# Fp32r matmuls of an encoder block: sixteen stationary tiles put 264 columns apart instead of 256, and attT on the weight tiles' remainder modulo 512 bytes

## The chip, the cores and the metric

The kernel runs on one core of one Trainium2 chip. The metric is the device time of one execution in microseconds (us); the times shown are of three executions.

## The reference

One layer of an encoder over 256 tokens with a model width of 2048, in float32:

```python
x = x + 0.5 * swiglu(rms_norm(x, norm_ffn1_w[l]), ffn1_w_gate[l], ffn1_w_up[l], ffn1_w_down[l])
x = x + head_group_mixer(rms_norm(x, norm_mix_w[l]), w_in[l], attn_sinks[l], ret_gn_w[l], w_out[l])
x = x + 0.5 * swiglu(rms_norm(x, norm_ffn2_w[l]), ffn2_w_gate[l], ffn2_w_up[l], ffn2_w_down[l])
...
return rms_norm(x, norm_final_w)
```

`swiglu` is `(silu(h @ w_gate) * (h @ w_up)) @ w_down` with an inner width of 5632. The mixer projects to 5376 columns, runs sliding-window attention (16 heads) on one half and retention (4 heads) on the other, and projects 2048 columns back with `w_out`.

## The kernel before, in words

Every large product is computed as three float32r matmuls per tile. An operand a is split into a high part and the remainder, a_lo = a - a_hi, and the product is a_hi·w_hi + a_hi·w_lo + a_lo·w_hi, all three accumulated in one PSUM bank. The helper `half` (lines 313 to 322) issues this for two k tiles (j) and two token tiles (t): 2 x 2 x 3 = 12 matmuls on lines 319, 320 and 321. In each, the **stationary** operand (what LDWEIGHTS puts into the array) is a 128 x 128 piece of the activations, and the **moving** operand is a row of 512 weight columns (448 in the input projection).

Four families of SBUF tiles hold the stationary pieces. `xT_hi` and `xT_lo` are the transposed, weighted x, 16 k tiles of 256 columns each; they serve gate, up and the input projection with tiles 0 to 15, and their upper eight tiles serve the retention half of `w_out`. `hT_hi` and `hT_lo` (4 k tiles) serve the down projections. `attT_hi` and `attT_lo` (8 k tiles) serve the attention half of `w_out` and, through `last_hT_hi` and `last_hT_lo`, the last down step of either FFN (`last_down`, lines 389 to 422, which in the second FFN issues its own matmuls on lines 419 to 421). A token tile is 128 float32 columns, 512 bytes, so t does not change an address modulo 512.

Weights come by DMA in pieces of 1 MB into `raw` (SP's queue, line 248), four slots; ScalarE copies half a slot into `w_hi` (line 613, rounding it to float32r) and VectorE subtracts to get `w_lo` (line 812). Both have four slots (`LEAD`), each of two rows of 512 columns, 2048 bytes a row. `half` waits on `lo_ready` for its slot and increments `half_used`, on which ScalarE waits before it overwrites the slot. The order of everything is written out by hand; TensorE runs gate and up of FFN step i, then down of step i - 1, with transposes (line 325) between them.

SBUF tensors are laid out one behind the other in the order in which `build` asks for them (line 77). The small tensors and the filler `to_line` end so that x, xT_hi, xT_lo, raw, w_hi and w_lo all begin at byte 0 modulo 512; each of these has a size that is a multiple of 512 bytes per partition. So have proj, cos, sin, junk, decay, hT_hi, hT_lo and the attention tiles behind them. The filler `off_line` (32 float32, 128 bytes) stands ahead of attT_hi, so attT_hi and attT_lo begin at byte 128 modulo 512.

Of the kernel before, what the change touches and what calls it, by code (L numbers as in the profile page):

```python
# [20 lines left out]
P = 128  # L21
D = 2048
SEQ = 256
T = SEQ // P
KT = D // P
# [17 lines left out]
RAW = 4  # L43
LEAD = 4
HALF = 2 * W


G_FFN = [0, 3 * NF + NI + 4]
# [19 lines left out]
F32R = mybir.dt.float32r  # L68
# [3 lines left out]
def build(nc, x_d, norms_d, g1, u1, d1, w_in, sinks_d, gn_d, w_out, g2, u2, d2, fw_d, ident_d, cos_d, sin_d,  # L72
          decay_d, out_d):
    ffn_w = [(g1, u1, d1), (g2, u2, d2)]
    with ExitStack() as ctx:
        def sb(name, shape, dt=F32, stack=ctx):
            return stack.enter_context(nc.sbuf_tensor(name, shape, dt))
# [23 lines left out]
        mv = sb("mv", [P, RH, T, 2])  # L101
        var_eps = sb("var_eps", [P, RH, T])
        gn_rstd = sb("gn_rstd", [P, RH, T])
        sb("to_line", [P, 32])


        x = sb("x", [P, T, D])
        xT_hi = sb("xT_hi", [P, KT, SEQ], F32R)
        xT_lo = sb("xT_lo", [P, KT, SEQ], F32R)
        raw = sb("raw", [P, RAW, 4 * W])  # L110
        w_hi = sb("w_hi", [P, LEAD, 2, W], F32R)
        w_lo = sb("w_lo", [P, LEAD, 2, W], F32R)
# [18 lines left out]
        probs = sb("probs", [P, T, QUAD, P])  # L131
        probsT = sb("probsT", [P, T, QUAD * P])
        att = sb("att", [P, T, QUAD * HD])
        sb("off_line", [P, 32])
        attT_hi = sb("attT_hi", [P, KT // 2, SEQ], F32R)
        attT_lo = sb("attT_lo", [P, KT // 2, SEQ], F32R)

# [94 lines left out]
        def f32(ap):  # L232
            return ap.bitcast(F32)
# [8 lines left out]
        def _(sp):  # L242
# [39 lines left out]
            for i, (kt0, kt1) in enumerate(X_PIECES):  # L282
                cols = slice(kt0 * P, kt1 * P)
                sp.dma_start(x[:, :, cols], xv[:, :, cols]).then_inc(x_loaded[i], 16)
                if i < 2:
                    sp.dma_start(raw[:, 0, i * HALF:(i + 1) * HALF].rearrange("p (k c) -> p k c", k=2),
                                 g1[2 * P * i:2 * P * (i + 1), 0:W].rearrange("(k p) c -> p k c", p=P)
# [313 lines left out]
        def _(act):  # L601
            def split(g, k, first=False):
# [9 lines left out]
                dst = w_hi[:, k % LEAD, :, :].rearrange("p k c -> p (k c)")  # L612
                act.activation(dst, raw[:, s, (k % 2) * HALF:(k % 2 + 1) * HALF], ACT.Copy).then_inc(hi_ready, 1)  # L613

# [191 lines left out]
        def _(dve):  # L806
            def split(g, k):
# [4 lines left out]
                dve.tensor_tensor(w_lo[:, k % LEAD, :, :].rearrange(flat),  # L812
                                  raw[:, k // 2, (k % 2) * HALF:(k % 2 + 1) * HALF],
                                  f32(w_hi[:, k % LEAD, :, :].rearrange(flat)), ALU.subtract).then_inc(lo_ready, 1)
# [364 lines left out]
```

## Time and profile before

| | |
|---|---|
| three runs, median (lowest to highest) | 1848.09 us (1847.88 to 1848.19) |
| the profiled execution's own time | 1848.02 us |
| its span, first to last instruction | 1846.2 us |
| mean granted TensorE clock | 0.999 |
| TensorE busy (PE) | 1835.1 us, 99% |
| weight loads busy (PEld, beside PE) | 1541.2 us, 83% |
| VectorE, ScalarE, GpSimd busy | 1045.5, 831.8, 64.2 us |
| HBM read | 341.95 MB, 186 GB/s over the span |

A row of a group of instructions gives line, engine, operation, output and inputs, shape and count, then the busy time in us and the mean duration of one in ns. Matmuls are pipelined, so a duration is longer than the distance to the next one; the distance from start to start is what one matmul costs, and the timeline view shows it.

### The profile page before, as it was taken

Reading aid. Unit: us, or ns where it says so; the run is one execution under the profiler, and the core shown is the slowest. Engines: PE = TensorE matmul, PEld = TensorE weight load, DVE = VectorE, ACT = ScalarE, POOL = GpSimd, SP = SyncE. Lnnn points to the kernel's source line nnn. Section 1 sums busy time; section 2 is a strip of 40 time slices with the busy share of each in tenths; the row PEclk is TensorE's granted clock in tenths of the full one; section 3 lists DMA queues with packets and bytes.
Section 4 is the critical chain, followed back from the end, with each engine's and each line's share of the span. In section 5 each row is a group of like instructions: output and inputs, shape, how many; then the busy total and the mean of one; then the engine's idle time right before and its main releaser. Section 6 shows DMA issues by size and latency. Waiting matters only on the chain.

```text
span 1846.2 us, 23124 instructions
## 1 busy us (share of the span) xinstructions
PE 1835.1 (99%) x8602; PEld 1541.2 (83%) x8602; DVE 1045.5 (57%) x1087; ACT 831.8 (45%) x995; POOL 64.2 (3%) x59
## 2 busy tenths in 40 slices
PE   9999999999999999999999999999999999999998
PEld 7888888888888888999998888888888888888886
DVE  5555565555556556655557665555555555546546
ACT  6444444444443444555555445443444444444344
POOL 0000000000000000000009000000000000000000
PEclk9999999999999999999999999999999999999999
DMA  8556556555555555564555456556556556555552
GB/s 312 192 183 200 185 184 202 182 191 195 184 195 190 187 198 173 165 194 160 163 174 177 140 171 210 190 183 202 183 185 201 182 192 194 184 193 190 189 198 92
DMA packets 176898, 344.53 MB, mean 187 GB/s; under 512 B 5984, under 2 KB 31456, under 8 KB 176736
## 3 DMA queue, kind: packets, MB, share of 16 engines
q1 hardware_dynamic: 176864, 344.07, 56.8%
q8 instruction: 23, 0.38, 0.1%
q14 instruction: 11, 0.09, 0.0%
HBM read 341.95 MB, written 2.10 MB: 186 GB/s over the span
## 4 chain that ended last, share of the span: by engine, by line
PE 99%; issue 0%; DMA 0%; DVE 0%; ACT 0%; SPq 0%; POOLq 0%; POOL 0%; DVEq 0%
PE ps L319 32%; PE ps L321 32%; PE ps L320 32%; PE ps L325 2%; PE ps L450 0%; PE ps L534 0%; PE ps L545 0%; DMA raw<-in_g 0%; PE ps L463 0%; PE ps L421 0%; PE ps L420 0%; PE ps L419 0%; DVE x L861 0%; DVE proj L1047 0%; DVE w_lo L812 0%
## 5 line engine op out<-in xcount | busy, mean ns | idle before, releaser
L812 DVE TENSOR_TENSOR w_lo<-raw,w_hi 128x1024 fp32r<-128x1024 f32 x656 | 812.8, 1241 | 762.4 <-ACT w_hi L613 761.2
L613 ACT ACTIVATE w_hi<-raw 128x1024 fp32r<-128x1024 f32 x656 | 695.2, 1061 | 972.8 <-PE ps L321 970.6
L319 PE MATMUL ps<-w_hi,xT_hi 128*128 128x512 f32 (+1 forms) x1856 | 718.3, 387 | 0.5 <-DVE w_lo L812 0.5
L321 PE MATMUL ps<-w_hi,xT_lo 128*128 128x512 f32 (+1 forms) x1856 | 713.3, 384 | 0.0
L320 PE MATMUL ps<-w_lo,xT_hi 128*128 128x512 f32 (+1 forms) x1856 | 713.1, 384 | 0.0
L319 PEld LDWEIGHTS ps<-w_hi,xT_hi 128*128 128x128 f32 x1856 | 348.6, 188 | 63.8 <-issue 1.9
L321 PEld LDWEIGHTS ps<-w_hi,xT_lo 128*128 128x128 f32 x1856 | 348.5, 188 | 63.3
L320 PEld LDWEIGHTS ps<-w_lo,xT_hi 128*128 128x128 f32 x1856 | 348.7, 188 | 61.7
L319 PE MATMUL ps<-w_hi,hT_hi 128*128 128x512 f32 x640 | 249.1, 389 | 0.0
L321 PE MATMUL ps<-w_hi,hT_lo 128*128 128x512 f32 x640 | 249.0, 389 | 0.0
L320 PE MATMUL ps<-w_lo,hT_hi 128*128 128x512 f32 x640 | 249.0, 389 | 0.0
L321 PEld LDWEIGHTS ps<-w_hi,hT_lo 128*128 128x128 f32 x640 | 120.2, 188 | 24.9
L320 PEld LDWEIGHTS ps<-w_lo,hT_hi 128*128 128x128 f32 x640 | 120.2, 188 | 24.8
L319 PEld LDWEIGHTS ps<-w_hi,hT_hi 128*128 128x128 f32 x640 | 120.2, 188 | 24.8
L861 DVE SCALAR_TENSOR_TENSOR x<-ps,x 128x512 f32<-128x512 f32 x188 | 120.3, 681 | 0.3 <-PE ps L321 0.3
L1054 POOL TENSOR_TENSOR rstd<-ms_eps,minus_half 128x2 f32<-128x2 f32 (+1 forms) x5 | 4.1, 827 | 1520.4 <-DVE ms_eps L835 1520.4
L319 PE MATMUL ps<-w_hi,attT_hi 128*128 128x512 f32 x112 | 45.9, 409 | 0.0
L321 PE MATMUL ps<-w_hi,attT_lo 128*128 128x512 f32 x112 | 44.2, 395 | 0.0
L320 PE MATMUL ps<-w_lo,attT_hi 128*128 128x512 f32 x112 | 44.2, 394 | 0.0
L824 DVE SCALAR_TENSOR_TENSOR xT_lo<-ps,norms,xT_hi 128x256 fp32r<-128x256 f32 x48 | 20.4, 477 | 20.0 <-ACT xT_hi L623 20.0
L845 DVE SCALAR_TENSOR_TENSOR h<-ps,rstd,sg 128x512 f32<-128x512 f32 x44 | 30.8, 742 | 0.0
L623 ACT ACTIVATE xT_hi<-ps,norms 128x256 fp32r<-128x256 f32 x48 | 19.3, 473 | 19.6 <-PE ps L325 19.6
(100 smaller groups left out, 526.0 us busy)
## 6 DMA issues: line engine op xcount, KB each, us to landing
raw<-in_u SPq DMA_DIRECT2D x88, 1024.0 KB, 5.1
raw<-in_d SPq DMA_DIRECT2D x88, 1024.0 KB, 4.9
raw<-in_g SPq DMA_DIRECT2D x87, 1024.0 KB, 5.1
raw<-in_w_in SPq DMA_DIRECT2D x48, 896.0 KB, 4.6
raw<-in_w_out SPq DMA_DIRECT2D x16, 1024.0 KB, 4.9
out<-proj SPq DMA_DIRECT2D x8, 256.0 KB, 2.4
x<-in_x SPq DMA_DIRECT2D x3, 512.0 KB, 9.5
raw<-in_g SPq DMA_DIRECT2D x2, 512.0 KB, 5.5
```

The source lines that it names most:

```text
L319: pe.matmul(out, xh, wh, start=first and j == 0, stop=False)
L320: pe.matmul(out, xh, wl, start=False, stop=False)
L321: mm = pe.matmul(out, xl, wh, start=False, stop=last and j == 1)
L325: return pe.transpose(ps[0:src.shape[1], bank, col:col + P], src, ident[:])
L613: act.activation(dst, raw[:, s, (k % 2) * HALF:(k % 2 + 1) * HALF], ACT.Copy).then_inc(hi_ready, 1)
L623: a = act.activation(xT_hi[:, kt, :], ps[:, x_bank(norm, p), j * SEQ:(j + 1) * SEQ], ACT.Copy, scale=norms[:, norm, kt:kt + 1])
L812: dve.tensor_tensor(w_lo[:, k % LEAD, :, :].rearrange(flat), raw[:, k // 2, (k % 2) * HALF:(k % 2 + 1) * HALF], f32(w_hi[:, k % LEAD, :, : ...
L824: a = dve.scalar_tensor_tensor(out=xT_lo[:, kt, :], in0=ps[:, x_bank(norm, p), j * SEQ:(j + 1) * SEQ], scalar=norms[:, norm, kt:kt + 1], i ...
L845: dve.scalar_tensor_tensor(out=h[:, t, :], in0=ps[:, B_UP + t, :], scalar=rstd[:, (FFN1, FFN2)[f], t:t + 1], in1=sg[:, t, :], op0=ALU.mult ...
L861: a = dve.scalar_tensor_tensor(out=xb, in0=ps[:, B_DOWN + 2 * (n % 2) + t, :], scalar=scale, in1=xb, op0=ALU.mult, op1=ALU.add)
L1054: pool.tensor_tensor(rstd[:, norm, t0:t1], ms_eps[:, norm, t0:t1], minus_half[:, t0:t1], ALU.pow).then_inc(rstd_ready, 1)
```

## The change

The rows of xT_hi and xT_lo become 264 columns (1056 bytes) long, of which the first 256 are used. k tile number n therefore begins 32·n bytes further modulo 512 than k tile 0. Both tensors grow by 16 x 32 = 512 bytes, so what stands behind them keeps its remainder relative to them. `to_line` loses 32 bytes, so x, xT_hi, xT_lo (tile 0), raw, w_hi, w_lo and the rest begin at byte 480 modulo 512. `off_line` goes, so attT begins at 480 too, as the weight tiles do. No instruction is added, removed or moved on any engine.

| | before, bytes modulo 512 | after |
|---|---|---|
| w_hi, w_lo, raw, hT, proj | 0 | 480 |
| xT, k tile n | 0 | 480 + 32·n |
| attT | 128 | 480 |
| xT relative to w | 0 | 32·n |
| hT relative to w | 0 | 0 |
| attT relative to w | 128 | 0 |

```diff
+STEP = 8
...
-        sb("to_line", [P, 32])
+        sb("to_line", [P, 24])
...
-        xT_hi = sb("xT_hi", [P, KT, SEQ], F32R)
-        xT_lo = sb("xT_lo", [P, KT, SEQ], F32R)
+        xT_hi = sb("xT_hi", [P, KT, SEQ + STEP], F32R)[:, :, 0:SEQ]
+        xT_lo = sb("xT_lo", [P, KT, SEQ + STEP], F32R)[:, :, 0:SEQ]
...
-        sb("off_line", [P, 32])
         attT_hi = sb("attT_hi", [P, KT // 2, SEQ], F32R)
         attT_lo = sb("attT_lo", [P, KT // 2, SEQ], F32R)
```

## Rows read from the trace of the kernel before

**Rows 1.** The page's first part and the granted clock by slice

```profile
PE 1835.1 (99%) x8602; PEld 1541.2 (83%) x8602; DVE 1045.5 (57%) x1087; ACT 831.8 (45%) x995; POOL 64.2 (3%) x59
...
PEclk9999999999999999999999999999999999999999
```

**Rows 2.** The chain that ended last, shares by engine and by line

```profile
PE 99%; issue 0%; DMA 0%; DVE 0%; ACT 0%; SPq 0%; POOLq 0%; POOL 0%; DVEq 0%
PE ps L319 32%; PE ps L321 32%; PE ps L320 32%; PE ps L325 2%; PE ps L450 0%; PE ps L534 0%; PE ps L545 0%; DMA raw<-in_g 0%; PE ps L463 0%; PE ps L421 0%; PE ps L420 0%; PE ps L419 0%; DVE x L861 0%; DVE proj L1047 0%; DVE w_lo L812 0%
```

**Rows 3.** Groups of instructions, shapes apart: matmuls by stationary tile

```profile
L319 PE MATMUL ps<-w_hi,xT_hi 128*128 128x512 f32 x1472 | 576.0, 391 | 0.5 <-DVE w_lo L812 0.5
...
L319 PE MATMUL ps<-w_hi,hT_hi 128*128 128x512 f32 x640 | 249.1, 389 | 0.0
...
L319 PE MATMUL ps<-w_hi,xT_hi 128*128 128x448 f32 x384 | 142.3, 371 | 0.0
...
L319 PE MATMUL ps<-w_hi,attT_hi 128*128 128x512 f32 x112 | 45.9, 409 | 0.0
...
L419 PE MATMUL ps<-w_hi,attT_hi 128*128 128x512 f32 x16 | 6.3, 394 | 0.0
```

**Rows 4.** Timeline (start us, duration us), a matmul beside the next load

```profile
1102.18 0.39 PE L319 MATMUL ps<-w_hi,xT_hi 128*128 128x512 f32 x1
1102.19 0.19 PEld L320 LDWEIGHTS ps<-w_lo,xT_hi 128*128 128x128 f32 x1
```

**Rows 5.** Timeline, TensorE: xT against w, first and last of 24 matmuls

```profile
1074.78 0.39 PE L320 MATMUL ps<-w_lo,xT_hi 128*128 128x512 f32 x1
...
1080.00 0.39 PE L319 MATMUL ps<-w_hi,xT_hi 128*128 128x512 f32 x1
```

**Rows 6.** Timeline, TensorE: hT against w, first and last of 24 matmuls

```profile
1399.68 0.39 PE L320 MATMUL ps<-w_lo,hT_hi 128*128 128x512 f32 x1
...
1404.90 0.39 PE L319 MATMUL ps<-w_hi,hT_hi 128*128 128x512 f32 x1
```

**Rows 7.** Timeline, TensorE: attT against w, first and last of 23 matmuls

```profile
1815.76 0.40 PE L319 MATMUL ps<-w_hi,attT_hi 128*128 128x512 f32 x1
...
1820.88 0.40 PE L320 MATMUL ps<-w_lo,attT_hi 128*128 128x512 f32 x1
```

**Rows 8.** Timeline, TensorE: attT in the first FFN, first and last of 14 matmuls

```profile
739.80 0.40 PE L320 MATMUL ps<-w_lo,attT_hi 128*128 128x512 f32 x1
...
742.84 0.39 PE L321 MATMUL ps<-w_hi,attT_lo 128*128 128x512 f32 x1
```

**Rows 9.** Timeline, TensorE: 448 columns, xT against w, first and last of 27

```profile
752.64 0.36 PE L321 MATMUL ps<-w_hi,xT_lo 128*128 128x448 f32 x1
...
757.91 0.36 PE L320 MATMUL ps<-w_lo,xT_hi 128*128 128x448 f32 x1
```

**Rows 10.** bf16 warm-up matmuls: three in the timeline, and the tile's durations (min/median/max ns)

```profile
8.25 0.81 PE L559 MATMUL ps<-junk 128*128 128x512 bf16 x3
...
L559 PE MATMUL ps<-junk x14: 379/631/631, 1.5 to 8.7; 128*128 128x512 bf16 x14
```

**Rows 11.** The two splits, and who waited for whom (us in total, times, longest)

```profile
L812 DVE TENSOR_TENSOR w_lo<-raw,w_hi 128x1024 fp32r<-128x1024 f32 x656 | 812.8, 1241 | 762.4 <-ACT w_hi L613 761.2
L613 ACT ACTIVATE w_hi<-raw 128x1024 fp32r<-128x1024 f32 x656 | 695.2, 1061 | 972.8 <-PE ps L321 970.6
...
ACT w_hi L613 <- PE ps L321: 970.6, 609, 3.5
...
ACT w_hi L613 <- DMA raw<-in_g: 0.7, 2, 0.4
...
raw<-in_u SPq DMA_DIRECT2D x88, 1024.0 KB, 5.1
```

## The prediction

> **What bounds the kernel now.** I read the page's first part first. TensorE is busy for 1835.1 us of the 1846.2 us span, and the granted clock is at its upper level, 2.4 GHz, in every slice [rows 1]. The chain of waits says the same: 99% of it lies on TensorE, and 96% on lines 319 to 321, the three products of `half` [rows 2]. So the time is the number of those matmuls times what one costs from start to start, and nothing that the change does elsewhere counts unless it comes to hold TensorE up.
>
> The groups with shapes kept apart give the numbers [rows 3]; each of the three lines has the same counts. Stationary from xT: 1472 x 3 = 4416 matmuls of 512 columns and 384 x 3 = 1152 of 448. From hT: 640 x 3 = 1920. From attT: 112 x 3 and, in the second FFN's last step, 16 x 3, together 384.
>
> The durations in these groups are of pipelined matmuls, so for the cost of one I go to the timeline and divide the distance between two starts by the number of steps:
>
> - xT, 512 columns: (1080.00 - 1074.78) / 23 = 0.2270 us [rows 5]
> - hT, 512 columns: (1404.90 - 1399.68) / 23 = 0.2270 us [rows 6]
> - attT, 512 columns: (1820.88 - 1815.76) / 22 = 0.2327 us [rows 7], and (742.84 - 739.80) / 13 = 0.2338 us in the first FFN [rows 8]
> - xT, 448 columns: (757.91 - 752.64) / 26 = 0.2027 us [rows 9], where 448/512 of 0.2270 would be 0.1986 us.
>
> This is the pair on which everything rests. hT and attT are used in down steps of the same shape, with the same moving operand and the same clock. They differ in where they stand: hT on the weight tiles' remainder modulo 512, attT 128 bytes past it. The second costs 5.7 ns more for each matmul. The timeline also shows why the two operands can meet: the load of the next stationary tile starts 0.01 us after the matmul it runs beside, and takes 0.19 of its 0.227 us [rows 4]. Both read SBUF at once.
>
> **The change, part by part.** No instruction is added or moved, so all of it is in the cost of one matmul.
>
> 1. *attT on the weights' remainder.* Its 384 matmuls come from 0.2327 to hT's 0.2270 us: 384 x 5.7 ns = 2.2 us less, all on the path. If another reason made attT slow, it is 0.
>
> 2. *xT's k tiles 1 to 15 off the weights' remainder*, by 32, 64, ... 480 bytes. Tile 0 stays on it. Gate and up take every tile equally often, and so does the input projection; the retention half of `w_out` takes tiles 8 to 15 alone. The matmuls of xT in the FFNs are 4416 less the 64 x 3 of `w_out`, 4224; with the projection's 1152 there are 5376, of which a sixteenth, 336, stays. So 5568 - 336 = **5232 matmuls** get a distance that is not 0.
>  Of the fifteen distances the trace shows one: 128, which is tile 4's, at 5.7 ns [rows 6, 7]. The bound above is worse than that: 0.2338 us, 6.8 ns for each [rows 5, 8], 5232 x 6.8 = 35.6 us. The bound below is a gain. The bf16 warm-up matmuls also stream 512 columns beside a load: three of them take 0.81 us with the last one's 0.379, so (0.81 - 0.379) / 2 = 0.2155 us [rows 10]. That is 11.5 ns below 0.2270, and 5232 x 11.5 = 60.2 us less if every distance reached it.
>  I take half of attT's price, 2.85 ns: among the distances some lie near 0 in either direction and some near or beyond 128, and the two that the trace shows cost 0 and 5.7. That is 5232 x 2.85 = **14.9 us more**, all on the path. For 448 columns I use the same figure; they already cost 4.1 ns more than in proportion [rows 5, 9], which says that a distance of 0 is no guarantee, and could cut both ways.
>
> 3. *Everything else now at remainder 480.* For hT the distance stays 0; I take 0. The splits on ScalarE and VectorE take 1061 and 1241 ns [rows 11] of the 12 x 0.227 = 2.72 us of a half, which leaves each of them over 1.4 us of a half, and ScalarE idles 970.6 us in all waiting for TensorE [rows 11]; either could take twice as long and stay hidden. If that cover went, TensorE would wait for `lo_ready`. A weight piece lands in 5.1 us, its slot is wanted again about six halves or 16 us later, and ScalarE waited only 0.7 us in all for one [rows 11]: a landing in raw at another remainder is hidden up to three times its time. ScalarE's and VectorE's writes of xT's tiles are one tile each, so the gaps cost them nothing; their bound is the same cover.
>
> The sum: 14.9 - 2.2 = +12.7 us. The profiled execution took 1848.02 us (span 1846.2 and 1.8 around it), as good as the median 1848.09, so 1848.1 + 12.7 = **1860.8 us**.
>
> One rule speaks against any effect. The Trainium skill, in "TensorE: Matmul & The Clock Gate" (step-by-step: what each phase is for), says that TensorE has two independent SBUF read ports, so that loading the next weights takes no read bandwidth from the running matmul; by it both terms would be 0 and the time 1848. The trace disagrees as far as its 5.7 ns between attT and hT go. The same page gives 215.7 ns between matmuls of 512 columns (back-to-back issue gap), and the warm-up's 0.2155 us agrees; the fp32r matmuls here stand 11 ns above it.
>
> **The rivals.**
>
> - *Every distance costs what 128 costs.* Then the term is 5232 x 5.7 = 29.8 us, the sum +27.6 and the time 1875.7 us. For it: attT is the one row off the remainder. Against: it is one distance of fifteen.
> - *The spread relieves the reads (faster).* At distance 0 the two streams start on the same remainder at the same moment [rows 4], and each of these matmuls stands 11.5 ns above the warm-up's. If that is a collision in each of them, some distances avoid it. With half of the matmuls, 2616, at 0.2155 us and the rest unchanged: 2616 x 11.5 = 30.1 us less, with attT's 2.2 less, 1815.8 us. It is decided by the mean over xT's distances: below 0.2270 us the kernel gains there, and with attT's part break-even lies 0.4 ns above it (2.2 / 5232). For it: nothing else in the rows explains why fp32r costs 11 ns more than bf16. Against: the only distance seen off 0 is worse, not better.
> - *The distance does nothing*, and attT is slow for a reason that goes with it or stays, such as its place far behind in SBUF. Then 1848.1 us, or 1845.9 with attT's part. Against it: nothing else differs between hT's and attT's matmuls.
> - *It is the remainder itself that counts, not the distance:* whatever does not begin at a multiple of 512 pays 5.7 ns. Then hT pays as well: (5568 + 1920) x 5.7 = 42.7 us, attT gains nothing, and the time is 1890.8 us. The rows can't exclude it, since all that stands at distance 0 also stands at byte 0.
> - That the change does not do what it says would need a tensor between xT and w_hi whose size is no multiple of 512; there is none (16896, 32768 and 16384 bytes).
>
> **How the numbers follow.** A measurement of this kernel can tell 0.2%, some 3.7 us, from no change. Forecast 0.33; every distance as 128: 0.17; relief 0.33; nothing 0.10; remainder itself 0.07. Faster is 0.33, within 0.2% 0.10, slower 0.33 + 0.17 + 0.07 = 0.57. Cases of both signs are open. The forecast's own range is 1850 to 1882 us (between hardly any cost and the upper bound, 1848.1 + 35.6 - 2.2 = 1881.5). The range of 8 in 10 reaches up to 1884 us, which leaves out the remainder itself (0.07), and down to 1812 us, which takes in the relief case down to a little below its worked value and leaves out the third of it, about 0.11, in which nearly every distance reaches the warm-up's figure.
>
> **What would show it.** In the changed kernel's timeline attT's matmuls should stand 0.227 us apart, and hT's still 0.227. Within a gate or up step the distance should change from one k tile to the next, since each brings 6 matmuls of one distance: tile 0 at 0.227, tile 4 near 0.233. A tile below 0.227 shows relief; all tiles at 0.233, the first rival; hT at 0.233, the remainder itself. VectorE's and ScalarE's splits should keep 1241 and 1061 ns. The prediction is wrong if the mean over the k tiles is below 0.2270 us, or if TensorE shows waits on `w_lo` that it does not have now.

## The result: 1.3% slower, and the profile after

| | before | after |
|---|---|---|
| runs, median (lowest to highest), us | 1848.09 (1847.88 to 1848.19) | 1872.66 (1872.51 to 1872.88) |
| ratio, with its 95% interval | | 1.0131 (1.0119 to 1.0144) |
| span of the profiled execution, us | 1846.2 | 1871.1 |

The changed kernel takes 24.6 us longer. It lies inside the range of 1812 to 1884 us, on the side that had 0.57, but twice as far from 1848 as the forecast of 1860.8 us. The first rival, every distance at attT's old price, gave 1875.7 us and is nearer.

The page of the kernel after shows the same amount of work in a longer span, at the same clock:

```profile
PE 1859.8 (99%) x8602; PEld 1541.0 (82%) x8602; DVE 1046.1 (56%) x1087; ACT 832.2 (44%) x995; POOL 63.3 (3%) x59
...
PEclk9999999999999999999999999999999999999999
...
L812 DVE TENSOR_TENSOR w_lo<-raw,w_hi 128x1024 fp32r<-128x1024 f32 x656 | 813.3, 1241 | 787.2 <-ACT w_hi L613 786.0
L613 ACT ACTIVATE w_hi<-raw 128x1024 fp32r<-128x1024 f32 x656 | 695.8, 1062 | 998.1 <-PE ps L321 995.0
```

TensorE has 24.7 us more busy time, the loads have none, and the two splits keep their 1241 and 1062 ns against [rows 11]. ScalarE's idle time in front of line 613 grew by 25 us: it waits longer for TensorE, as everything does. So the cost lies in the matmuls alone.

The timeline of TensorE of the kernel after, one up projection of the second FFN. These are the starts of k tiles 0, 1, 6, 7, 14 and 15 (6 matmuls each) and, behind them, the first matmul of the down step:

```profile
1661.60 0.40 PE L319 MATMUL ps<-w_hi,xT_hi 128*128 128x512 f32 x1
...
1662.99 0.40 PE L319 MATMUL ps<-w_hi,xT_hi 128*128 128x512 f32 x1
...
1669.98 0.40 PE L319 MATMUL ps<-w_hi,xT_hi 128*128 128x512 f32 x1
...
1671.36 0.40 PE L319 MATMUL ps<-w_hi,xT_hi 128*128 128x512 f32 x1
...
1681.15 0.40 PE L319 MATMUL ps<-w_hi,xT_hi 128*128 128x512 f32 x1
...
1682.53 0.40 PE L319 MATMUL ps<-w_hi,xT_hi 128*128 128x512 f32 x1
...
1683.93 0.40 PE L319 MATMUL ps<-w_hi,hT_hi 128*128 128x512 f32 x1
```

The same pass of the kernel before:

```profile
1638.99 0.39 PE L319 MATMUL ps<-w_hi,xT_hi 128*128 128x512 f32 x1
...
1660.75 0.39 PE L319 MATMUL ps<-w_hi,hT_hi 128*128 128x512 f32 x1
```

The pass of 96 matmuls took 21.76 us, 0.2267 us each, and now takes 22.33 us, 0.2326 us each. Within it the price follows the tile. Tile 6 (192 bytes off) has 1.38 / 6 = 0.230 us and tile 14 (448 bytes off) the same; tile 15 has 1.40 / 6 = 0.233. Tile 0, whose distance is 0, has 1.39 / 6 = 0.232 and not 0.2267. There are 44 such passes (gate and up, 11 steps, two FFNs): 44 x 0.57 = 25.1 us by this one pass. Over all passes of the kernel after, tile 0 has a mean of 229.9 ns and tile 8, which is 256 bytes off, 231.1; tile 4, 128 bytes off, has 232.5, and in the kernel before the mean over all tiles is 226.9 (gaps over 300 ns, in which TensorE waited or did something else, left out).

The tiles with the unchanged distance, and attT. First hT in a down step of the kernel after (34 matmuls), then attT in the last step of the second FFN (first and last of 22):

```profile
1428.79 0.39 PE L321 MATMUL ps<-w_hi,hT_lo 128*128 128x512 f32 x1
...
1436.27 0.39 PE L321 MATMUL ps<-w_hi,hT_lo 128*128 128x512 f32 x1
...
1841.23 0.39 PE L319 MATMUL ps<-w_hi,attT_hi 128*128 128x512 f32 x1
...
1845.99 0.39 PE L319 MATMUL ps<-w_hi,attT_hi 128*128 128x512 f32 x1
```

hT stands at 7.48 / 33 = 0.2267 us as in [rows 6], although it now begins at byte 480. attT went from 0.2327 us [rows 7] to 4.76 / 21 = 0.2267.

Summed over the whole of either trace, each matmul counted from its start to the next one's start (so with what waiting there was), the families have:

| stationary tile, moving columns | before, us | after, us | difference, us |
|---|---|---|---|
| xT, 512 (4416 matmuls) | 1005.1 | 1029.9 | +24.8 |
| xT, 448 (1152) | 236.5 | 237.1 | +0.7 |
| hT, 512 (1920) | 435.4 | 436.0 | +0.6 |
| attT, 512 (383 of 384 are in the trace) | 90.7 | 89.2 | -1.5 |

Together +24.6 us. The profiled spans differ by 24.9, and the other 0.3 us lie in the warm-up matmuls ahead of the work.

### The profile page after: what moved, and what is told of

It is laid out like the page before. It is cut to its first block, busy times and chain, and to the rows that moved or that the text cites. A ratio compares the mean times of both kernels' runs of the same rounds, so it can differ in the third digit from the quotient of the medians.

```text
span 1871.1 us, 23124 instructions
## 1 busy us (share of the span) xinstructions
PE 1859.8 (99%) x8602; PEld 1541.0 (82%) x8602; DVE 1046.1 (56%) x1087; ACT 832.2 (44%) x995; POOL 63.3 (3%) x59
## 4 chain that ended last, share of the span: by engine, by line
PE 99%; issue 0%; DMA 0%; DVE 0%; ACT 0%; SPq 0%; POOLq 0%; POOL 0%; DVEq 0%
PE ps L319 32%; PE ps L321 32%; PE ps L320 32%; PE ps L325 2%; PE ps L450 0%; DMA raw<-in_g 0%; PE ps L534 0%; PE ps L545 0%; PE ps L463 0%; PE ps L421 0%; PE ps L419 0%; PE ps L420 0%; DVE x L861 0%; DVE proj L1047 0%; DVE w_lo L812 0%
## 5 line engine op out<-in xcount | busy, mean ns | idle before, releaser
L812 DVE TENSOR_TENSOR w_lo<-raw,w_hi 128x1024 fp32r<-128x1024 f32 x656 | 813.3, 1241 | 787.2 <-ACT w_hi L613 786.0
L613 ACT ACTIVATE w_hi<-raw 128x1024 fp32r<-128x1024 f32 x656 | 695.8, 1062 | 998.1 <-PE ps L321 995.0
L319 PE MATMUL ps<-w_hi,xT_hi 128*128 128x512 f32 (+1 forms) x1856 | 727.0, 392 | 0.4 <-DVE w_lo L812 0.4
L321 PE MATMUL ps<-w_hi,xT_lo 128*128 128x512 f32 (+1 forms) x1856 | 721.7, 389 | 0.0
```

Source lines behind the costliest of these rows:

```text
L319: pe.matmul(out, xh, wh, start=first and j == 0, stop=False)
L321: mm = pe.matmul(out, xl, wh, start=False, stop=last and j == 1)
L812: dve.tensor_tensor(w_lo[:, k % LEAD, :, :].rearrange(flat), raw[:, k // 2, (k % 2) * HALF:(k % 2 + 1) * HALF], f32(w_hi[:, k % LEAD, :, : ...
```

## The experiments

All runs were compared with the kernel before on the same chip; its median was 1848.28, 1848.56 and 1848.26 us in the three groups of runs. Times are medians, except that each run with added series is one execution, read from its trace alone.

### Parts of the change, one at a time

**attT's share alone.**

```diff
-        sb("off_line", [P, 32])
```

> The filler ahead of attT goes and nothing else: attT at distance 0 from the weight tiles, xT at distance 0 as before. Theory A (the distance between stationary and moving operand modulo 512 bytes sets the cost of a matmul): attT's 384 matmuls come from 0.2325 to about 0.227 us, the kernel to 1845.9 us, and this is the share of the changed kernel's time that was a gain. Rival B (attT was slow for its place or for its neighbours in the program): nothing changes, 1848.1 us.

Measured: 1846.9 us against 1848.28, ratio 0.9991 (0.9982 to 1.0). Its timeline has attT, first and last of 24 matmuls, 5.21 / 23 = 0.2265 us apart:

```profile
1814.73 0.39 PE L318 MATMUL ps<-w_hi,attT_hi 128*128 128x512 f32 x1
...
1819.94 0.39 PE L320 MATMUL ps<-w_hi,attT_lo 128*128 128x512 f32 x1
```

The price per matmul moved as theory A has it. The total gained 1.4 us where 2.2 were expected, and the interval of the ratio just reaches 1, so the total alone would not settle it. The trace does: from start to start attT's matmuls take 89.1 us in all instead of 90.7, 1.6 us less. (All matmul lines stand one line higher here, since one line of the source is gone.)

**Everything at byte 480, all distances 0.**

```diff
-        sb("to_line", [P, 32])
+        sb("to_line", [P, 24])
...
-        sb("off_line", [P, 32])
```

> As the run before it, and to_line 32 bytes shorter, so that x, xT, raw, w_hi, w_lo, hT, attT all begin at byte 480 modulo 512, at distance 0 from each other. Theory A (distance alone): the same as the run before it, 1845.9 us. Rival C (it is the remainder 480 itself that costs): matmuls at 0.2327 us everywhere, about +43 us, near 1889 us. The changed kernel's hT at 0.227 us speaks for A already.

Measured: 1848.46 us, ratio 1.0001 (0.9992 to 1.001), with single runs from 1847.58 to 1850.69. Rival C falls: nothing near 43 us. It is 1.6 us above the run before it, which theory A did not have. In the profiled executions the distance is 3.1 us (1849.51 and 1846.37), and it lies in the 448-column matmuls, which take 239.6 us in all instead of 236.6. There are 30 steps between these two rows of the timeline, 0.2067 us each:

```profile
769.77 0.37 PE L318 MATMUL ps<-w_hi,xT_hi 128*128 128x448 f32 x1
...
775.97 0.37 PE L318 MATMUL ps<-w_hi,xT_hi 128*128 128x448 f32 x1
```

The kernel before has 0.2027 for the same shape at the same distance [rows 9]. This second price of one geometry comes back in the series below.

**All xT tiles at one distance, 256 bytes.**

```diff
+        sb("gap", [P, 64])
         raw = sb("raw", [P, RAW, 4 * W])
...
-        sb("off_line", [P, 32])
```

> xT's tiles stand 256 columns apart as before, all sixteen at one distance of 256 bytes from the weight tiles (a filler of 256 bytes between xT_lo and raw); attT and hT at distance 0. Theory A: xT's matmuls of 512 columns at about 0.2325 us, 4416 x 5.7 ns = +25 us on the run with attT alone, near 1871 us. Rival D (the price of the changed kernel comes from the change of distance between one k tile and the next, not from the distance): 0.227 us for xT, 1846 us. Rival E (half way round the line the two reads are farthest apart and don't meet): xT's matmuls below 0.227 us, down to 0.216, 1846 - 49 = 1797 us.

Measured: 1846.78 us, ratio 0.9992 (0.9983 to 1.0001). In its trace the matmuls of xT with 512 columns take 1005.1 us, as in the run with attT alone (1005.0). By itself this looked like rival D, and the theory that any distance costs 5.7 ns was wrong. The series settled which.

### The price of each distance

**Series with fixed distances.** Behind the last down step, TensorE goes on with matmuls on what the weight buffers hold; their results are left out of the output:

```diff
             ffn(1)
+            def series(cols, offs, n, still=P):
+                for c in offs:
+                    for i in range(n):
+                        pe.matmul(ps[0:still, i % 2, 0:cols], w_hi[:, 0, 0, c:c + still], w_lo[:, 1, 0, 0:cols],
+                                  start=True, stop=True)
+            series(512, range(0, 136, 8), 32)
+            series(448, range(0, 136, 8), 24)
+            series(512, range(1, 8), 24)
+            series(512, (0,), 24, 64)
```

> The kernel before with extra fp32r matmuls on TensorE behind its last down step (their result is not used, the total time is some 260 us longer and says nothing). Each series has one distance between the stationary tile (128 columns of w_hi) and the moving row (w_lo): 0, 32, 64, ... 512 bytes with 32 matmuls of 512 columns each, the same distances with 24 of 448 columns each, then 4, 8, ... 28 bytes with 24 of 512 columns, then distance 0 with a stationary tile of 64 columns. Theory A: 0.227 us at 0 and 512 bytes, about 0.232 at all others. Rival D: 0.227 at every distance, since none changes within a series. Rival E: a curve with a low place, below 0.227, somewhere. With 64 stationary columns, if it is the load's reads that the moving operand meets, about half of the 11 ns above the warm-up's 0.2155 us should go: 0.221 us; if fp32r has a fixed cost, 0.227.

The timeline merges the matmuls of one line, so a window over the settled part of a series gives one row: start, then the time from its first start to its last end. With the last one's 0.39 us (512 columns) taken off and the rest divided by the count less one, that is the price. The 512-column series at 0, 32, 64, 96, 128, 160, 192, 224 and 256 bytes:

```profile
1840.39 5.84 PE L602 MATMUL ps<-w_lo,w_hi 128*128 128x512 f32 x25
...
1847.69 5.99 PE L602 MATMUL ps<-w_lo,w_hi 128*128 128x512 f32 x25
...
1855.16 5.99 PE L602 MATMUL ps<-w_lo,w_hi 128*128 128x512 f32 x25
...
1862.62 6.01 PE L602 MATMUL ps<-w_lo,w_hi 128*128 128x512 f32 x25
...
1870.10 5.97 PE L602 MATMUL ps<-w_lo,w_hi 128*128 128x512 f32 x25
...
1877.54 5.99 PE L602 MATMUL ps<-w_lo,w_hi 128*128 128x512 f32 x25
...
1884.97 5.89 PE L602 MATMUL ps<-w_lo,w_hi 128*128 128x512 f32 x25
...
1892.33 5.99 PE L602 MATMUL ps<-w_lo,w_hi 128*128 128x512 f32 x25
...
1899.75 5.84 PE L602 MATMUL ps<-w_lo,w_hi 128*128 128x512 f32 x25
```

| distance, bytes | 0 | 32 | 64 | 96 | 128 | 160 | 192 | 224 | 256 |
|---|---|---|---|---|---|---|---|---|---|
| 512 columns, ns | 227.1 | 233.3 | 233.3 | 234.2 | 232.5 | 233.3 | 229.2 | 233.3 | 227.1 |

From 256 to 512 bytes the rows repeat to the hundredth of a microsecond. So distance does have a price, also where it never changes, and rival D falls as the only cause. But the price repeats every **256 bytes, not 512**; that is why the kernel with 256 bytes lost nothing. With 512 columns no distance that was tried is cheaper than 0. Distances of 4 to 28 bytes cost 230.6 to 235.0 ns, so 32 bytes is not the grain either. The 232.5 ns at 128 bytes are attT's old 232.7 [rows 7]; the mean over eight steps of 32 bytes is 232.0 ns.

A series needs some matmuls to settle. The first six steps of the series at distance 0 take 235, 225, 230, 236, 229 and 232 ns, 231.2 on average, before it comes down to 226.7.

With 448 columns, at 0, 96, 192 and 256 bytes:

```profile
1965.99 3.82 PE L602 MATMUL ps<-w_lo,w_hi 128*128 128x448 f32 x18
...
1980.61 3.77 PE L602 MATMUL ps<-w_lo,w_hi 128*128 128x448 f32 x18
...
1995.24 3.76 PE L602 MATMUL ps<-w_lo,w_hi 128*128 128x448 f32 x18
...
2005.20 3.67 PE L602 MATMUL ps<-w_lo,w_hi 128*128 128x448 f32 x17
```

With 0.36 us taken off [rows 9] these are 0.2035, 0.2006, 0.2000 and 0.2069 us. Here 0 is not the best distance, and 0 and 256 differ though 512 columns treat them alike. The settled gaps show how: at 256 bytes they repeat as 206, 207, 207 ns (mean 206.7), at 0 as 199, 207, 203, 202, 203 and so on (mean 202.7).

A stationary tile of 64 columns at distance 0 cost 0.2307 us (3.85 us for 16), more than one of 128. Halving what the load reads does not shorten the matmul, so the expected 0.221 is wrong.

**More series.** `one(i, s0, cols, still, m0)` is one fp32r matmul with a stationary tile of `still` columns at column s0 of w_hi and the moving row at column m0 of w_lo; `bf` is the same for bf16, its distance being 2·s0 bytes.

```diff
             ffn(1)
...
+            for s0 in (0, 16, 64):
+                for i in range(24):
+                    bf(i, s0)
...
+            for i in range(24):
+                one(i, 64 * (i % 2))
+            for i in range(24):
+                one(i, 8 * (i % 2))
+            for kt in range(32):
+                for i in range(6):
+                    one(i, 8 * (kt % 16))
+            for cols in (480, 384, 320, 256):
+                for i in range(24):
+                    one(i, 0, cols)
+            for i in range(24):
+                one(i, 24, 448)
+            for i in range(48):
+                one(i, 0, 448)
+            for i in range(24):
+                one(i, 64, 448)
...
```

> The kernel before with other series of matmuls behind its last down step (results unused; the total says nothing). In order: bf16 operands at distances 0, 64, 256 bytes: if only fp32r reads meet the load, all three at 0.2155 us. fp32r of 512 columns with the stationary tile alternately at distances 0 and 256: 0.2267 us if the curve has a period of 256 bytes. Alternately 0 and 32: between 0.2267 and 0.2332. Six matmuls at each of 0, 32, ... 480 in turn, as the changed kernel has them, 192 in all: 0.2319 us if the price is the mean of the curve over its distances, 0.2325 as in the changed kernel if moving from one distance to another costs something of its own. 480, 384, 320, 256 columns at distance 0: in proportion to the columns (0.2125, 0.170 ...) or not below the load's 0.19. 448 columns at distance 0 after a series at 96 and after one at 256: 0.2029 and 0.2064 if the cost hangs on what came before. 448 columns with both operands moved by 64 bytes (distance 0), then the moving one alone (distance 192): 0.203 or 0.206, then 0.2002. A stationary tile of 32 columns at distance 0: 0.2267 if the load's length has no part.

Rows of its timeline, in this order: bf16 at distance 0 and at the next one (32 bytes, where the expectation says 64); 0 and 256 in turn; 0 and 32 in turn; six matmuls at each of 0, 32, ... 480; 384 columns, as two windows; 256 columns, as two windows; 448 columns at 96 bytes:

```profile
1840.11 3.83 PE L604 MATMUL ps<-w_lo,w_hi 128*128 128x512 bf16 x17
...
1845.29 3.83 PE L604 MATMUL ps<-w_lo,w_hi 128*128 128x512 bf16 x17
...
1860.98 4.02 PE L600 MATMUL ps<-w_lo,w_hi 128*128 128x512 f32 x17
...
1866.47 4.16 PE L600 MATMUL ps<-w_lo,w_hi 128*128 128x512 f32 x17
...
1872.09 43.21 PE L600 MATMUL ps<-w_lo,w_hi 128*128 128x512 f32 x185
...
1921.39 3.28 PE L600 MATMUL ps<-w_lo,w_hi 128*128 128x384 f32 x18
...
1922.77 0.68 PE L600 MATMUL ps<-w_lo,w_hi 128*128 128x384 f32 x3
...
1928.73 2.32 PE L600 MATMUL ps<-w_lo,w_hi 128*128 128x256 f32 x18
...
1929.81 0.52 PE L600 MATMUL ps<-w_lo,w_hi 128*128 128x256 f32 x3
...
1932.12 3.87 PE L600 MATMUL ps<-w_lo,w_hi 128*128 128x448 f32 x18
```

- bf16 costs (3.83 - 0.38) / 16 = 0.2156 us at either distance. The price of distance is one of fp32r.
- 0 and 256 in turn: (4.02 - 0.39) / 16 = 0.2269 us. Going back and forth between two distances of the low price costs nothing. As the price repeats every 256 bytes, this does not say what a change between two different prices costs; the next line does.
- 0 and 32 in turn: 0.2356 us, above both 0.2271 and 0.2333, where the expectation had a value between them. The change itself costs here.
- The changed kernel's pattern: (43.21 - 0.39) / 184 = **0.2327 us**, where the kernel has 0.2326 and the mean of the curve is 0.2320. So the order of distances, with nothing else of the kernel around it, makes the price. Some 0.6 ns come from moving between them.
- 384 columns: (3.28 - 0.68) / 15 = 0.1733 us; 256 columns: (2.32 - 0.52) / 15 = 0.1200 us. At 2.4 GHz these columns take 160 and 106.7 ns, and 512 take 213.3. Each is 13.3 ns below the measured price. Between 256 and 512 columns the price grows by 106.7 ns, 0.417 ns for a column, which is just 2.4 GHz. At distance 0 the excess is the same for every one of these widths: a fixed cost of an fp32r matmul here, which does not grow with what the moving row reads.
- 448 columns at 96 bytes had 0.2065 us this time and 0.2006 in the series before; at 256 bytes 0.203 here and 0.2069 there. One geometry has two prices.
- A stationary tile of 32 columns cost 0.232 us, and 480 columns 0.2169, 16.9 ns above their 200, so the 13.3 ns do not hold for every width.

The order of the program does not fix which of the two prices holds. The kernel before and the run with the first series are the same program up to the added matmuls. Yet at the same place in the input projection, first and last of 24 matmuls, the kernel before has 4.66 / 23 = 0.2026 us and that run 4.76 / 23 = 0.2070. First the kernel before, then the run with the first series:

```profile
841.36 0.36 PE L319 MATMUL ps<-w_hi,xT_hi 128*128 128x448 f32 x1
...
846.02 0.36 PE L321 MATMUL ps<-w_hi,xT_lo 128*128 128x448 f32 x1
...
841.79 0.37 PE L319 MATMUL ps<-w_hi,xT_hi 128*128 128x448 f32 x1
...
846.55 0.37 PE L321 MATMUL ps<-w_hi,xT_lo 128*128 128x448 f32 x1
```

So small differences in time between two executions can bring either price. The 3 us between executions of the kernel with everything at byte 480 are of the size that this makes; only one of its executions has a trace, so that is an inference.

**The moving row moved.**

```diff
             ffn(1)
...
+            for m0 in range(0, 64, 8):
+                for i in range(24):
+                    one(i, 0, m0)
+            for b in (8, 16, 24, 48):
+                for i in range(24):
+                    one(i, b, b)
+            for i in range(24):
+                one(i, 16 * (i % 2), 16 * (i % 2))
+            for i in range(24):
+                one(i, 16 * (i % 2), 16 * ((i + 1) % 2))
```

> The kernel before with a third set of series behind its last down step (results unused). Stationary tile at byte 0, moving row at 0, 32, 64, ... 224 bytes, 24 matmuls of 512 columns each: if the difference alone counts, the earlier curve backwards: 0.2267 at 0, 0.2332 at 32, 0.2292 at 64, 0.2331 at 96, 0.2323 at 128, 0.2340 at 160, 0.2334 at 192, 0.2332 at 224 us; if it is the stationary tile's own remainder, 0.2267 at all of them. Then both at 32, 64, 96, 192 bytes: 0.2267 if the difference alone counts. Then both changing together between 0 and 64 from one matmul to the next, and then in opposite turns: a load that runs beside a moving row at the other remainder in the first case (distance 64 and 192 in turn), at the same one in the second; if what counts is the distance between a row and the load beside it (that of the next matmul), the second is 0.2267 us and the first near 0.231; if it is the distance within a matmul, the other way round.

Rows: the moving row at 32 and 64 bytes, both at 96, both changing together, both in opposite turns.

```profile
1845.66 4.13 PE L600 MATMUL ps<-w_lo,w_hi 128*128 128x512 f32 x17
...
1851.24 4.06 PE L600 MATMUL ps<-w_lo,w_hi 128*128 128x512 f32 x17
...
1895.70 4.02 PE L600 MATMUL ps<-w_lo,w_hi 128*128 128x512 f32 x17
...
1906.67 4.10 PE L600 MATMUL ps<-w_lo,w_hi 128*128 128x512 f32 x17
...
1912.24 3.90 PE L600 MATMUL ps<-w_lo,w_hi 128*128 128x512 f32 x16
```

The moving row 64 bytes ahead costs 0.2294 us, like the stationary tile 192 bytes ahead, and 32 bytes ahead 0.2338, like 224. The other five places of the moving row cost 0.2338 to 0.2344, within 1.5 ns of the curve read backwards. Both operands at 96 bytes cost 0.2269, and so do both at 32, 64 and 192. For a repeated pair it is the difference that counts. The last two series were to say which load a row must agree with, the one beside it or its own; they gave 0.2319 and 0.2340 us, neither of them 0.2267. Both readings fail as they were put, and how the two streams hinder each other stays open. No run has matmuls without a load beside them, so that it is the load's reads that meet the moving row's is argued from [rows 4], not shown.

### The curve in the kernel

**xT 192 bytes off, uniformly.** The filler of the run with 256 bytes, now of 16 columns:

```diff
+        sb("gap", [P, 16])
         raw = sb("raw", [P, RAW, 4 * W])
...
-        sb("off_line", [P, 32])
```

> As the run with attT alone, and a filler of 64 bytes between xT_lo and raw: all xT tiles 192 (448) bytes ahead of the weight tiles modulo 256 (512), uniformly. By the series: 512 columns 0.2292 us, 4416 x 2.5 ns = +11.0 us; 448 columns 0.2002 instead of 0.2028, 1152 x -2.6 ns = -3.0 us; together 1846.9 + 8.0 = 1854.9 us. Rival D (only the change of distance costs): 1846.9 us.

Measured: 1853.38 us, ratio 1.0027 (1.0016 to 1.0037). Its up pass in the timeline takes 21.98 / 96 = 0.2290 us:

```profile
1644.96 0.39 PE L319 MATMUL ps<-w_hi,xT_hi 128*128 128x512 f32 x1
...
1666.94 0.40 PE L319 MATMUL ps<-w_hi,hT_hi 128*128 128x512 f32 x1
```

The series' 0.2292 carries over. A uniform distance, with no change from tile to tile, costs time in the kernel too: xT's matmuls of 512 columns take 10.1 us more in all than before, those of 448 columns 3.1 us less.

**Only xT_hi staggered.**

```diff
-        xT_hi = sb("xT_hi", [P, KT, SEQ], F32R)
+        xT_hi = sb("xT_hi", [P, KT, SEQ + STEP], F32R)[:, :, 0:SEQ]
...
-        sb("off_line", [P, 32])
```

> Only xT_hi has its tiles 264 columns apart; xT_lo keeps distance 0, to_line is as before, off_line is gone. Two of three loads have the distances of the changed kernel. If each load pays by its own distance: two thirds of 5.7 ns per matmul of 512 columns, 4416 x 3.8 = +16.8 us, 1863.7 us. If any change of distance from one load to the next unsettles the next matmuls: the whole 25 us or more, 1872 us or above. If only uniform distances are cheap because hi and lo agree, more still.

Measured: 1868.36 us, ratio 1.0107 (1.0091 to 1.0122), between the two numbers. The up pass:

```profile
1657.80 0.39 PE L319 MATMUL ps<-w_hi,xT_hi 128*128 128x512 f32 x1
...
1680.08 0.39 PE L319 MATMUL ps<-w_hi,hT_hi 128*128 128x512 f32 x1
```

22.28 / 96 = 0.2321 us: 5.4 of the 5.9 ns are there with two thirds of the loads moved, and over the whole trace 22.1 of the 24.8 us. The third load, at distance 0 between two that are not, pays as well. It fits 0 and 32 in turn, which cost more than either.

### A version faster than both

**448 columns at distance 192, the rest at 0.** Only the input projection changes: its weight columns stand 64 bytes into their rows.

```diff
+SHIFT = 16
...
-                dst = raw[:, s, :].rearrange("p (k c) -> p k c", k=4)[:, :, 0:width]
+                o = SHIFT if width == WI else 0
+                dst = raw[:, s, :].rearrange("p (k c) -> p k c", k=4)[:, :, o:o + width]
...
+                o = SHIFT if width == WI else 0
...
-                        wh, wl = (w[:, k % LEAD, j, 0:width] for w in (w_hi, w_lo))
+                        wh, wl = (w[:, k % LEAD, j, o:o + width] for w in (w_hi, w_lo))
...
-        sb("off_line", [P, 32])
```

> As the run with attT alone, and in the input projection the 448 weight columns stand in columns 16 to 463 of their row instead of 0 to 447 (raw, w_hi and w_lo alike), so only these matmuls get distance 192. By the series 0.2002 us instead of 0.2028: 1152 x 2.6 ns = 3.0 us less, 1843.9 us, faster than both kernels. If the series don't carry over to the kernel: 1846.9 us.

Measured: 1843.38 us, ratio 0.9972 (0.9962 to 0.9983). The timeline has 31 steps between these rows, 6.20 / 31 = 0.2000 us:

```profile
769.66 0.36 PE L321 MATMUL ps<-w_hi,xT_hi 128*128 128x448 f32 x1
...
775.86 0.36 PE L322 MATMUL ps<-w_lo,xT_hi 128*128 128x448 f32 x1
```

1152 x (0.2027 - 0.2000) = 3.1 us, and attT's 1.6 by its trace, make 4.7 us, which is the difference of the profiled spans (1846.2 and 1841.5). The medians differ by 5.2.

**The same at distance 96** (`SHIFT = 40`).

> As the run with the 448 columns shifted, but by 40 columns (160 bytes), so that xT stands 96 bytes ahead of them modulo 256, the other low place of the series (0.2002 us). The same time as there, 1843.4 us, if the curve holds; 1846.9 us if only distance 192 is good in the kernel; above 1848 us if the curve is of no use off its measured points.

Measured: 1844.49 us, ratio 0.9979 (0.997 to 0.9988). Nearly as good, and above its sibling by 1.1 us, all of it in the 448-column matmuls (234.5 us in all against 233.4). A distance with two prices in the series is the less safe choice.

## Why the prediction was right, point by point

- **What bounds the kernel:** right. TensorE holds 99% of either span, and the whole difference of 24.9 us in span is in its busy time (24.7 us).
- **Term 1, attT:** right in mechanism (0.2327 to 0.2267 us); 2.2 us was worked out, 1.4 measured alone, 1.6 by that run's trace.
- **Term 2, xT off the weights' remainder:** right in sign, wrong in size. This is the term that was mis-sized: "I take half of attT's price, 2.85 ns" over 5232 matmuls, 14.9 us. The 4416 matmuls of 512 columns pay 5.6 ns on average, 24.8 us, and the 1152 of 448 columns 0.7 us: 25.5 us in all. The reason given for the half, distances that lie near 0, doesn't hold: 4 bytes already cost 232.5 ns, and of the steps of 32 bytes only 0 and 192 modulo 256 are low.
- **The count:** the price was taken to repeat every 512 bytes, so only tile 0 was to be spared. It repeats every 256, which puts tile 8 at distance 0 too, and neither is spared: they have 229.9 and 231.1 ns, not 0.227 us as forecast for tile 0. Six matmuls are hardly enough to settle, as the 231.2 ns of a series' first six steps show.
- **The 448 columns** were given the same 2.85 ns on 1080 matmuls, 3.1 us. They cost 0.7: 30 steps from 769.73 to 775.81 us in the kernel after are 0.2027, as before. In the series the eight steps of 32 bytes have a mean of 202.9 ns at 448 columns, next to 202.7 at distance 0. So 448 columns at distance 0 were never at their best, which the prediction saw as "no guarantee".
- **Term 3:** right in the main. hT at byte 480 costs 0.2267 us once settled (0.6 us more over its 1920 matmuls, where 0 was taken), the splits and landings (5.2 us against 5.1) stay hidden, and the run with all at 480 shows no 43 us.
- The sum now reads 24.8 + 0.7 + 0.6 - 1.5 = +24.6 us; the medians differ by 24.6. The forecast had half of it. That the time lies in the range owes much to the range's width, from 36 us faster to 36 us slower; a third of the chances went to a faster kernel, so even the direction was held with little confidence.
- **The rivals.** Every distance as 128 was the nearest, with 0.17 where it deserved more: the only row off distance 0 was typical of the fifteen, and I discounted it for no row. Relief is out for 512 columns: none of the distances tried costs less than 0 does, and the 11 ns above the warm-up's figure are there at the best distance too. For 448 columns there is a relief of 2.7 ns, which the last two runs take. No effect and the remainder itself are out.

The Trainium skill's rule that the load takes no read bandwidth from the running matmul ("TensorE: Matmul & The Clock Gate", step-by-step: what each phase is for) holds for bf16 here (0.2156 us at either distance), not for fp32r, where the place that the load reads from is worth up to 7 ns of 227. The same page's 215.7 ns at 512 columns agrees with the bf16 series; fp32r has 226.7.

## What to carry to other kernels

With fp32r matmuls of 512 columns in a row, each with its own load, let the stationary tile and the moving row begin at the same remainder modulo 256 bytes, for all operand families, and pad no tile of one by a few bytes; attT's case shows how one group of 384 matmuls at another remainder can be found in a trace by its distance from start to start. Where the moving row has 448 columns, try other distances: a few series behind the kernel's last matmul price all of them in one run. When one row of a trace shows the price of a condition, take it whole until another row speaks against it.

## What the runs showed that was not expected

- The price of a distance repeats every 256 bytes: at 512 columns the series from 256 on are those from 0 on (5.84, 5.99, 5.99, 6.01 us ...).
- An fp32r matmul of 256, 384 or 512 columns at distance 0 costs 13.3 ns more than its columns take at 2.4 GHz; bf16 costs 2.3 ns more.
- A 256-column fp32r matmul goes every 0.120 us although each load is shown as lasting 0.19 us, so the load's shown duration is no bound on the distance between two.
- At 448 columns one geometry has two prices (0.203 and 0.207 us at distance 0, 0.2006 and 0.206 at 96), and two executions of the same instructions can differ in it. What holds it in one or the other was not found, nor how load and row hinder each other.
